# Two output stages: the first four row tiles summed together, weight chunk by weight chunk, and loads four tiles ahead queued in front of a store

## What is computed

```python
# first block: oa, ob are attention outputs already gated
y = jnp.concatenate([oa, ob], axis=-1) @ w_out[l]
x = x + gate[:, None, :] * rms_norm(y, g_post[l])

# second block: a is gated, r still has to be
r = rms_norm_2(r, ...).reshape(B, E, HGRN_WIDTH) * jax.nn.silu(gate_h)
y = jnp.concatenate([a, r], axis=-1) @ w_out[l]
h = layer_norm(DN_ALPHA * h + y, ln_g[l], ln_b[l])
```

## Time and profile before

| | |
|---|---|
| median of 3 runs | 3702.32 us (3697.86 to 3705.59) |
| profiled execution | 3703.39 us, its span 3701.7 us |
| TensorE matmul busy | 3338.0 us, 90% |
| VectorE busy | 1987.3 us, 54% |
| ScalarE busy | 1405.9 us, 38% |
| GpSimd busy | 946.2 us, 26% |
| matmuls of L850, three groups of 512 | 202.4 + 200.9 + 200.7 us busy |
| granted TensorE clock, mean | 0.95 |

### The profile page before, as it was taken

How to read it: one execution, slowest core, us unless ns; L and a number is a source line. 1 busy time by engine, 2 the same in 40 slices (tenths; PEclk the granted TensorE clock), 3 DMA queues, 4 the chain that set the end, 5 groups by cost and what they waited for, 6 DMA issues and landing times. The chain is left out here.

```text
span 3701.7 us, 44032 instructions
## 1 busy us (share of the span) xinstructions
PE 3338.0 (90%) x15859; PEld 2526.3 (68%) x15906; DVE 1987.3 (54%) x3662; ACT 1405.9 (38%) x2382; POOL 946.2 (26%) x862
## 2 busy tenths in 40 slices
PE   6899999899999997895789999997995999999698
PEld 4689888656666665784567787886773666666387
DVE  4200011267666665432289998975672565556366
ACT  3200001134444444212157998342553333333344
POOL 0120111257455451101322233444232112111100
PEclk8999999899999998997899999998997999999799
DMA  6221223466554532445211235454135324222344
GB/s 227 66 82 58 71 76 117 121 141 139 111 122 105 111 88 91 129 131 211 66 52 47 78 102 182 124 166 156 65 110 158 102 64 95 59 55 59 104 152 128
DMA packets 336734, 399.79 MB, mean 108 GB/s; under 512 B 105430, under 2 KB 254262, under 8 KB 323944
## 3 DMA queue, kind: packets, MB, share of 16 engines
q1 hardware_dynamic: 258380, 281.28, 27.4%
q10 hardware_dynamic: 71552, 78.03, 7.1%
q0 software_dynamic: 6592, 37.75, 3.6%
HBM read 264.35 MB, written 132.62 MB: 107 GB/s over the span
## 5 line engine op out<-in xcount | busy, mean ns | idle before, releaser
L2209 PE MATMUL f_pO<-f_PT,f_vv 128*128 128x512 f32 (+3 forms) x944 | 381.8, 487 | 20.8 <-ACT f_PT L2239 20.8
L2301 DVE TENSOR_REDUCE f_mxc<-f_pM 128x1 f32<-128x512 f32 (+2 forms) x448 | 240.0, 541 | 221.0 <-PE f_pM L2133 127.6
L2239 ACT ACTIVATE f_PT<-f_pS 128x512 f32<-128x512 f32 (+3 forms) x472 | 221.8, 473 | 352.5 <-PE f_pS L2172 171.9
L2651 PE MATMUL cbank<-hT_high,cw_hi 128*128 128x512 f32 x800 | 319.3, 399 | 29.8 <-POOL cw_lo L2604 25.3
L2306 DVE CUSTOM_DVE_ANT_0 n_junk<-n_pM,n_chosen 128x512 bf16<-128x512 f32 (+4 forms) x352 | 200.1, 571 | 270.6 <-PE n_pM L2139 137.6
L2841 DVE TENSOR_SCALAR_CACHE_REDUCE sharedI<-xI,TI 128x768 bf16<-128x768 f32 (+10 forms) x276 | 339.6, 1296 | 5.4 <-DVE TI L2846 5.2
L590 PE MATMUL p_bank<-hT_high,p_w_hi 128*128 128x512 f32 (+1 forms) x768 | 304.8, 397 | 33.1 <-POOL p_w_lo L556 28.1
L2239 ACT ACTIVATE n_PT<-n_pS 128x512 f32<-128x512 f32 (+4 forms) x352 | 177.5, 504 | 388.2 <-PE n_pS L2189 319.2
L2651 PE MATMUL cbank<-hT_low,cw_hi 128*128 128x512 f32 x800 | 316.0, 395 | 0.0
L2651 PE MATMUL cbank<-hT_high,cw_lo 128*128 128x512 f32 x800 | 315.8, 395 | 0.0
L2209 PE MATMUL n_pO<-n_PT,n_vv 128*128 128x512 f32 (+4 forms) x704 | 305.6, 515 | 3.9 <-issue 1.3
(11 more groups left out here) (415 smaller groups left out, 7480.8 us busy)
## 6 DMA issues: line engine op xcount, KB each, us to landing
cw_raw<-in_w_in_dram SPq DMA_DIRECT2D x50, 512.0 KB, 4.7
f_zz<-scratch_z ACTq DMA_DIRECT2D x128, 128.0 KB, 3.0
p_w_raw<-in_w_in_dram SPq DMA_DIRECT2D x23, 512.0 KB, 3.9
wa<-in_w_ada_dram SPq DMA_DIRECT2D x8, 1024.0 KB, 6.1
xt<-in_x_dram SPq DMA_DIRECT2D x16, 512.0 KB, 7.2
scratch_z<-p_stage ACTq DMA_DIRECT2D x32, 256.0 KB, 2.4
scratch_qk_high<-p_stage ACTq DMA_DIRECT2D x32, 256.0 KB, 2.5
scratch_qk_low<-p_stage_low ACTq DMA_DIRECT2D x32, 256.0 KB, 3.2
```

The source lines that it names most:

```text
L2209: pe.matmul(pO[:, B % 2, c0:c1], lhsT=vv[0:nk, b, kt, :], rhs=PT[0:nk, u % PR, c0:c1], start=(kt == 0 and not heads[h].local), stop=(heads ...
L2239: act.activation(PT[0:nk, u % PR, c0:c1], pS[0:nk, u % SR, c0:c1], ACT.Exp, scale=0.125).then_inc(s_ex, 1)
L2301: v.tensor_reduce(to, pM[:, n % 2, 0:wd], AX.X, ALU.max).then_inc(s_mx, 1)
L2651: last = pe.matmul(bank[:, p % RING, 0:wd], lhsT=w_part[pw][b][:, c, :], rhs=rhs, start=(c == 0 and a == 0), stop=(c == DC - 1 and a == 2))
```

## The change

- TensorE: tiles 0 to 3 are summed together. The loop over weight chunks k is outside, the loop over the four tiles inside; for each chunk TensorE waits for that chunk's w_lo, and with chunk 0 for each tile's low part. Tiles 4 to 15 go as before, one by one; a tile waits for the finished tile four before.
- pY has four buffers of 1024 columns, G_hi and G_lo have four each. gT, xg, og, zg, g1 keep two.
- w_out is loaded in eight pieces of 512 KB.
- ScalarE and VectorE: one order by hand, `in_order`. The weight chunks 0 to 3 are made behind the split (high or low) of the tiles 0 to 3, the others after that; gate(n + 1) comes right after split(n) (before the first split both gate(0) and gate(1)), and finish is two turns behind, with tiles 0 and 1 finished in turn 4, and 2 and 3 in turn 5.
- SyncE: parts and gT of tiles 0 and 1, xg of 0 and 1, parts and gT of 2 to 5; then for each tile n the loads of n + 4, the store of n, xg of n + 2 (tile 6 in turn 0, tile 7 in turn 2).

```diff
-        pY = m.ps(n_("pY"), [P, 2, D])
+        pY = m.ps(n_("pY"), [P, 4, D])
...
+        FIRST = 4
+        def in_order(gate, split, finish, weight):
+            for n in range(FIRST):
+                for g in ((0, 1) if n == 0 else (n + 1,)):
+                    gate(g)
+                split(n)
+                weight(n)
+            for k in range(FIRST, DC):
+                weight(k)
+            for n in range(FIRST, NT + 2):
+                if n < NT:
+                    split(n)
+                if n + 1 < NT:
+                    gate(n + 1)
+                for t in {FIRST: (0, 1), FIRST + 1: (2, 3)}.get(n, (n - 2,)):
+                    finish(t)
...
-            parts = ((3, load_parts),) if part is not None else ()
-            skeleton(parts + ((2, load_turned), (-1, store), (1, load_rows)))
+            for n in range(2):
+                load(n)
+            for n in range(2):
+                load_rows(n)
+            for n in range(2, 6):
+                load(n)
+            for n in range(NT):
+                for t in {0: (6,), 1: (), 2: (7,), 3: ()}.get(n, (n + 4,)):
+                    if t < NT:
+                        load(t)
+                store(n)
+                if n + 2 < NT:
+                    load_rows(n + 2)
...
-            for k in range(0, DC, 2):
-                gp.dma_start(wraw[:, k:k + 2, :], w_out[0, k * P:(k + 2) * P, :].rearrange("(k p) n -> p k n", p=P)
-                             ).then_inc(s_w[k // 2], 16)
-            split_low(gp, 1)
+            for k in range(DC):
+                gp.dma_start(wraw[:, k, :], w_out[0, k * P:(k + 1) * P, :]).then_inc(s_w[k], 16)
+            for k in range(1, DC, 2):
+                weight_low(gp, k)
...
+            for k in range(DC):
+                pe.wait_ge(s_wl[k % 2], k // 2 + 1)
+                for n in range(FIRST):
+                    if k == 0:
+                        pe.wait_ge(s_lo, n + 1)
+                    for z in range(2):
+                        last = products(n, k, z)
+                    if k == DC - 1:
+                        last.then_inc(s_y, 1)
+            for n in range(FIRST, NT):
                 pe.wait_ge(s_lo, n + 1)
-                pe.wait_ge(s_res[b], r)
+                pe.wait_ge(s_res[n % 2], n // 2 - 1)
...
-                if n >= 2:
-                    act.wait_ge(s_y, n - 1)
+                if n >= 4:
+                    act.wait_ge(s_y, n - 3)
...
-            skeleton(((1, high), (-1, finish)) + (((2, gate),) if part is not None else ()))
+            in_order(gate, high, finish, weight)
```

More of the change, by code:

```diff
@@ L757, in stage_out @@
             sig = m.sb(n_("sig"), [P, HW])
-        G_hi = [m.sb(n_(f"Ghi{i}"), [P, DC, P], F32R) for i in range(2)]
-        G_lo = [m.sb(n_(f"Glo{i}"), [P, DC, P], F32R) for i in range(2)]
+        G_hi = [m.sb(n_(f"Ghi{i}"), [P, DC, P], F32R) for i in range(4)]
+        G_lo = [m.sb(n_(f"Glo{i}"), [P, DC, P], F32R) for i in range(4)]
         junk = m.sb(n_("junk"), [P, D])
@@ L822, in store, with load @@
                 sp.dma_start(rows_out[ds(n * P, P), :], tt[:, b, :]).then_inc(s_st[b], 16)
-            parts = ((3, load_parts),) if part is not None else ()
-            skeleton(parts + ((2, load_turned), (-1, store), (1, load_rows)))
+            def load(n):
+                if part is not None:
+                    load_parts(n)
+                load_turned(n)
+            for n in range(2):
[4 more added lines that the diff above has]
+                load(n)
@@ L843, in _, with products @@
         def _(pe):
-            def multiply(n, b, r):
+            def products(n, k, z):
+                for a, (pg, pw) in enumerate(PASSES):
+                    last = pe.matmul(pY[:, n % 4, z * HW:(z + 1) * HW], lhsT=(G_hi, G_lo)[pg][n % 4][:, k, :],
+                                     rhs=(w_hi, w_lo)[pw][:, k, z * HW:(z + 1) * HW],
+                                     start=(k == 0 and a == 0), stop=(k == DC - 1 and a == 2))
+                return last
+            for k in range(DC):
[7 more added lines that the diff above has]
+                        last.then_inc(s_y, 1)
@@ L853, in multiply, with weight, gate @@
                 last.then_inc(s_y, 1)
-            for z in range(2):
-                pe.wait_ge(s_wl[z], DC // 2)
-            skeleton(((0, multiply),))
         @block.scalar
         def _(act):
-            for k in range(DC):
-                act.wait_ge(s_w[k // 2], 16)
+            def weight(k):
+                act.wait_ge(s_w[k], 16)
                 act.activation(w_hi[:, k, :], wraw[:, k, :], ACT.Copy).then_inc(s_wh, 1)
-            def gate(n, b, r):
+            def gate(n):
+                if part is None:
+                    return
+                b, r = n % 2, n // 2
@@ L867, in gate, with high, finish @@
                 act.activation(sig[:], zg[:, b, :], ACT.Sigmoid).then_inc(s_sig, 1)
-            def high(n, b, r):
+            def high(n):
+                b, r, c = n % 2, n // 2, n % 4
                 act.wait_ge(s_gt[b], r * 16 + 16)
-                if n >= 2:
-                    act.wait_ge(s_y, n - 1)
-                last = act.activation(G_hi[b][:, 0:GIVEN], gT[:, b], ACT.Copy)
+                if n >= 4:
+                    act.wait_ge(s_y, n - 3)
+                last = act.activation(G_hi[c][:, 0:GIVEN], gT[:, b], ACT.Copy)
                 if part is not None:
                     act.wait_ge(s_gated, n + 1)
-                    last = act.activation(G_hi[b][:, GIVEN:].rearrange("p a b -> p (a b)"), g1[:, b, :], ACT.Copy)
+                    last = act.activation(G_hi[c][:, GIVEN:].rearrange("p a b -> p (a b)"), g1[:, b, :], ACT.Copy)
                 last.then_inc(s_hi, 1)
-            def finish(n, b, r):
+            def finish(n):
+                b = n % 2
                 if ln:
@@ L893, in _, with weight, gate @@
             own_ = Tally(v, s_dve)
-            split_low(v, 0)
-            def gate(n, b, r):
+            def weight(k):
+                if k % 2 == 0:
+                    weight_low(v, k)
+            def gate(n):
+                if part is None:
+                    return
+                b, r = n % 2, n // 2
                 v.wait_ge(s_in[b], r * 32 + 32)
@@ L947, in _ @@
                 v.wait_ge(s_c, 32)
-            skeleton(((1, low), (-1, finish)) + (((2, gate),) if part is not None else ()))
+            in_order(gate, low, finish, weight)
 def stage_turn(nc, used, rows, meta, blocks, hT_meta, HT):
```

54 lines of the change are left out of this document (26 added, 28 removed).

## The result

The changed kernel takes 3719.22 us (median of six runs against 3704.18 for the kernel before in the same comparison), 15.0 us more. One of the six took 8531.49 us, for which nothing on record gives a cause, and the ratio leaves it out; the median of the other five is 3719.08. The profiled execution took 3719.08 us against 3703.39, 15.7 more.

The account below looks back on a forecast made before the run. After start-up, TensorE was taken to bound stage 1, with waits through VectorE and ScalarE slowing stage 2. Stage 1 -2.0 and stage 2 +11.2 made +9.2 us: 3712.6 profiled, 3711.5 median, range 3699.5 to 3719.5.

Parts of the forecast that it names:

- stage 1, start-up: Before 24 matmul slots of stage 1 are done: done at about 1494.0 instead of 1498.75, -4.7 us.
- stage 2, start-up: Before 24 matmul slots of stage 2 are done: ScalarE's gates wait for queued loads ahead of weights, +4.2 us.
- stage 2, gap before tile 4: TensorE in stage 2 waits for finish(0), which follows gate(5) on VectorE: +8.1 us, the clock falling to 1.2 GHz.
- stage 2, tile 6 with half clock: TensorE in stage 2 waits for low(6) behind VectorE's finishes; the wait swallows the half clock: +3.8 us in all.
- stage 2, ring: VectorE's per-tile chain in stage 2 drops from 11.27 to 10.57 us, under TensorE's 10.88: -4.9 us.
- Steady tiles: After the start, gate(n + 1) before finish(n - 2) lets TensorE set the pace at 10.88 us a tile; stage 1 unchanged.
- The clock survives it: Stage 1, 2.7 us gap before tile 4: the clock was expected to stay at 2.4 GHz.
- The queue: During start-up, queues alternate packet by packet, so 512-byte rows lose eight to one against the weights' 4 KB rows.
- U: Time when 24 slots of stage 2 are done: 3520.5 to 3523.7, taken as 3522.0, against 3517.8 before.
- Rival 1: Start-ups shorten as drawn, no engine waiting behind a load: stage 1 -10, stage 2 +0.2 us, 3692.5 us; chance 0.07.
- rivals 3 and 4: Split loads lose rate, 3718.5 us, chance 0.08; engine order isn't had, VectorE's period stays 11.27 us, 3716.4 us, chance 0.05.
- Rival 2: Stage 2's start-up costs about nothing and stage 1 gains 4: +3 us, 3705.5; chance 0.32 for all within 0.2%.

Follow-up runs that it names:

- e7: Changed kernel with no tiles summed together: all eight weights first, then tiles one by one, new gate and finish order kept; 3699.78 us, 0.9986 of before.
- e3: Changed kernel with only tile 0 summed chunk by chunk, the other tiles one by one, finish(n - 2) every turn; 3680.85 us, 0.9951 of before.
- e9: Changed kernel with finish(0) before gate(5) in turn 4, and later gates behind finish; 3725.97 us, 1.0065 of before.
- e10: Changed kernel, GpSimd's chunks 3, 5, 7 after low(3), gate(n + 1) behind weight(n), gain and offset loaded later; 3712.38 us, 1.0023 of before.
- e5: Changed kernel with only tile 0 summed chunk by chunk, all weights before gate(1), gain and offset loaded behind first parts and gT; 3675.80 us, 0.9918 of before.
- e1: Changed kernel, but GpSimd makes w_lo of chunks 3, 5 and 7 only after low(3); 3714.37 us, 1.0039 of before.
- e6: Kernel before with only w_out split into eight loads of 512 KB; 3699.21 us, 0.9988 of before.
- e11: Changed kernel, but xg of tiles 0 and 1 queued behind the loads of tiles 2 and 3; 3718.06 us, 1.0041 of before.

## Why the prediction was right or wrong

| term | forecast | trace |
|---|---|---|
| stage 1, start-up | -4.7 | -4.7 (matmul 25: 32.06 to 27.40 after the first issue) |
| stage 1, gap before tile 4 | +2.7 | +2.7 (and no half clock behind it, see below) |
| stage 2, start-up | +4.2 | +8.5 (35.30 to 43.83) |
| stage 2, half clock behind matmul 24 | none | +1.3 |
| stage 2, gap before tile 4 | +8.1 | +8.1 |
| stage 2, tile 6 with half clock | +3.8 | +3.4 (3573.01 to 3598.15, less 96 x 0.2267) |
| stage 2, ring | -4.9 | -4.9 |
| sum of the stages | +9.2 | +14.6 |
| the rest of the program | 0 | +1.1 |

(The terms of the trace add up to 14.4; 0.2 is rounding and half clock behind the gaps.)

- Steady tiles: right, and shown alone by e7. VectorE's pace was forecast at 10.57 us a tile; behind tile 4 of the changed kernel its last step of a tile starts every 10.47 or 10.48 us.
- Gaps: right to a few tenths; e3, where they are gone, and e9 and e10, where they stay, show that they come from holding four tiles open, since VectorE may finish none until tile 0's last chunk.
- "The clock survives it", said of stage 1's gap, came true in the changed kernel's profiled execution by luck. Behind the same gap of 2.7 us the clock was at its lower level in the other five executions that have it, for 1.4 to 1.7 us more. With it stage 1 was no shorter than before (199.8 to 201.0 us against 200.5) where its start-up was the changed kernel's, so the forecast of -2.0 was met in one execution of five; the start-up itself was 4.0 to 4.8 us shorter in all five.
- The queue: packet by packet, eight to one. The landing of zg 4 was forecast at 3515.9; counted from the same start it came at 3514.43 + 0.78 = 3515.2, and high(2) of stage 1 began at 1488.11 - 0.83 = 1487.3 with gT 2 forecast at 1486.5. e5 shows the cause by putting the small rows ahead.
- The term that was mis-sized is stage 2's start-up, in its last link. The prediction wrote "3.2 more to low(3)" and "up to 2 more" for products beside GpSimd's subtractions, and took U (when 24 slots are done) at 3522.0. It had the row (2.83 us where 0.69 is usual) and charged it as one instruction's share. But low(3) is two instructions that fall just when ScalarE runs through weights 3 to 7 and GpSimd has three subtractions back to back: each waited one out, 4.3 us in all, and e1 takes them away. From the sigmoid of gate(4) to the end of low(3) it was 8.4 us, and 3.7 in e1. U was 3525.57 + 0.78 = 3526.35, outside the 3520.5 to 3523.7 given for it.
- With TensorE idle before tile 3 the clock was at its lower level when chunk 1 began: matmuls went on at 0.43 us until 3528.14. That is the 1.3 us; the prediction ran all 150 slots from U to T at 0.2267 us and had no term for it.
- The "about 400" GB/s that the prediction gives the 1 MB loads is the sum of both queues in the earlier trace rows; the weights alone moved 0.36 MB in that microsecond. The sum uses 0.40 for both queues together, so nothing in it changes.
- Rival 1 (the start-ups shorten as drawn) is met in stage 1 only in part (4.7 of 12.7 us), rivals 3 and 4 are refuted by e6 and e7. Rival 2, within 0.2%, would have needed this start-up term at nothing.

Still open: why the first half-clock stretch of stage 1 differs between executions of the same stage (11 to 20 matmuls), why the clock fell behind the gap of 2.7 us in five executions and not in the sixth, and what the collision of low(3) with GpSimd costs on average over the runs, since only profiled executions show it.

## What to carry to other kernels

Summing several tiles together while weights come in keeps the matmul engine busy, but it also holds back whatever finishes a tile; where the finishing engine needs nearly a tile's time per tile (10.5 us against 10.9 here), a group of one is enough, and the group of four costs 8.1 and 3.4 us behind its end in the second stage, 2.7 in the first. When an instruction's time is taken from a row, see what else runs beside it at its new place: two-input VectorE operations next to a stream of GpSimd subtractions have to be priced at up to the other's full length, each. And put small-row loads that start a stage in the queue before the large ones flow, not vectors that are wanted last.

## What the runs showed of the hardware that was not expected

- VectorE's 0.69 us subtraction took 2.85 and 2.83 us when one of GpSimd's (2.37 and 2.79 us) had started 0.06 and 0.51 us before it; in e1 the same took 0.68.
- Eight weight loads of 512 KB were no slower than four of 1 MB: the last one landed 17.0 and 17.3 us after the first issue where it was 17.0 and 18.1, and the first matmul came 1.3 and 1.8 us sooner (e6).
- Behind a gap of 2.7 us before tile 4 of stage 1 matmuls started 0.227 us apart in one execution (granted clock 1.00, 2.4 GHz) and 0.43 apart, 5 to 8 of them, in five others (0.50, 1.2 GHz, in the rows of e11). Behind the 8.07 us of stage 2 it was 0.43 in all five executions that have that gap, for 6 to 12 matmuls.
